# Four adaLN gate groups of the second layer: summed on VectorE in the first layer's output projection, not multiplied on TensorE in the second layer

## What is computed

```python
for l in range(DEPTH):
    last = l == DEPTH - 1
    shift, scale, gate = jnp.split(jax.nn.silu(c) @ ada_w[l] + ada_b[l], 3, axis=-1)
    shift_c, scale_c, gate_c = jnp.split(jax.nn.silu(c_ctx) @ ada_w[l] + ada_b[l], 3, axis=-1)
    h = rmsnorm(x, norm_g[l]) * (1.0 + scale[:, None]) + shift[:, None]
    hc = rmsnorm(xc, norm_g[l]) * (1.0 + scale_c) + shift_c
    ...                       # projections, attention, pooling, Fourier mixing
    x_new = x + gate[:, None] * out
    if not last:
        ...
        xc = xc + gate_c * outc
    x = x_new
```

## Time and profile before

| | |
|---|---|
| median of 3 runs | 2350.83 us (2349.53 to 2353.44) |
| span of the profiled execution | 2348.8 us |
| TensorE busy (matmul) | 2272.0 us, 97% |
| VectorE busy | 1288.4 us, 55% |
| ScalarE busy | 1042.1 us, 44% |
| GpSimd busy | 269.0 us, 11% |
| DMA | 437.14 MB, mean 186 GB/s |

### The profile page before, as it was taken

One profiled execution on the slowest core, in us unless ns is written; L12 is line 12 of the kernel. 1 busy time (PEld: TensorE's weight loads), 2 busy tenths in 40 slices (PEclk: granted clock), 3 DMA queues, 4 the chain that ended last, 5 costly groups with the idle time before them and its releaser, 6 DMA issues.

```text
span 2348.8 us, 30025 instructions
## 1 busy us (share of the span) xinstructions
PE 2272.0 (97%) x11859; PEld 1830.4 (78%) x11859; DVE 1288.4 (55%) x2030; ACT 1042.1 (44%) x1596; POOL 269.0 (11%) x326
## 2 busy tenths in 40 slices
PE   5899999999999999999999998999999999999998
PEld 2477777777777867678888887888888888888887
DVE  3354523332332264555776776667765777567764
ACT  2233333332322255445554565555544555345553
POOL 1010100000010122100020324111100111001111
PEclk9999999999999999999999998999999999999999
DMA  9974433445655475634566544565655555555553
GB/s 350 341 263 157 149 126 114 139 132 167 243 179 172 134 276 194 237 96 159 181 207 204 172 143 153 179 196 180 189 195 190 187 185 184 198 188 188 188 189 116
DMA packets 322427, 437.14 MB, mean 186 GB/s; under 512 B 13848, under 2 KB 220112, under 8 KB 321264
## 3 DMA queue, kind: packets, MB, share of 16 engines
q1 hardware_dynamic: 316800, 413.19, 53.2%
q0 software_dynamic: 3392, 16.90, 1.9%
q10 hardware_dynamic: 2096, 5.15, 0.6%
HBM read 428.89 MB, written 6.29 MB: 185 GB/s over the span
## 4 chain that ended last, share of the span: by engine, by line
PE 87%; DVE 4%; ACT 3%; DMA 3%; issue 1%; POOL 1%; SPq 0%; ACTq 0%; POOLq 0%
PE ps L1334 24%; PE ps L1335 12%; PE ps L1309 9%; PE ps L1311 8%; PE ps L1310 8%; PE ps L1329 5%; PE ps L1330 5%; PE ps L1331 5%; PE ps L1289 3%; PE ps L1383 1%; DVE SPL L1784 1%; ACT SPL L1540 1%; PE ps L1400 1%; DMA RAW<-in_ada_w_dram 1%; PE ps L1390 1%
## 5 line engine op out<-in xcount | busy, mean ns | idle before, releaser
L1784 DVE TENSOR_TENSOR SPL<-RAW,SPL 128x1024 fp32r<-128x1024 f32 x592 | 751.6, 1274 | 598.4 <-ACT SPL L1540 596.1
L1334 PE MATMUL ps<-HS,SPL 128*128 128x512 f32 x2688 | 957.7, 401 | 10.8 <-DVE SPL L1784 7.8
L1540 ACT ACTIVATE SPL<-RAW 128x1024 fp32r<-128x1024 f32 x592 | 622.1, 1055 | 493.2 <-PE ps L1311 170.9
L1335 PE MATMUL ps<-HS,SPL 128*128 128x256 f32 x2688 | 755.3, 281 | 0.0
L1334 PEld LDWEIGHTS ps<-HS,SPL 128*128 128x128 f32 x2688 | 507.7, 189 | 135.4 <-DVE SPL L1784 5.6
L1335 PEld LDWEIGHTS ps<-HS,SPL 128*128 128x128 f32 x2688 | 510.5, 190 | 2.0 <-issue 1.7
L1309 PE MATMUL ps<-SPL,HS 128*128 128x512 f32 x960 | 396.8, 413 | 12.2 <-DVE SPL L1784 5.3
L1311 PE MATMUL ps<-SPL,HS 128*128 128x512 f32 x960 | 377.1, 393 | 0.0
L1310 PE MATMUL ps<-SPL,HS 128*128 128x512 f32 x960 | 376.9, 393 | 0.0
L1309 PEld LDWEIGHTS ps<-SPL,HS 128*128 128x128 f32 x960 | 182.1, 190 | 75.5 <-issue 17.5
L1310 PEld LDWEIGHTS ps<-SPL,HS 128*128 128x128 f32 x960 | 182.3, 190 | 41.8 <-issue 6.3
(11 more groups left out here) (281 smaller groups left out, 1689.3 us busy)
## 6 DMA issues: line engine op xcount, KB each, us to landing
RAW<-in_w_in_dram SPq DMA_DIRECT2D x208, 512.0 KB, 5.7
RAW<-in_ada_w_dram SPq DMA_DIRECT2D x192, 512.0 KB, 4.9
RAW<-in_ffn_w_up_dram SPq DMA_DIRECT2D x192, 512.0 KB, 3.5
RAW<-in_w_out_dram SPq DMA_DIRECT2D x96, 512.0 KB, 4.5
RAW<-in_ffn_w_down_dram SPq DMA_DIRECT2D x96, 512.0 KB, 4.1
x_spill<-XT POOLq DMA_DIRECT2D x2, 2048.0 KB, 15.3
XT<-x_spill POOLq DMA_DIRECT2D x1, 4096.0 KB, 17.4
MM<-in_x_dram ACTq DMA_DIRECT2D x2, 1024.0 KB, 10.8
```

The costliest lines, as they stand in the source:

```text
L1334: mm(PS[b][:, :], wr, hh, start=k == 0, stop=False, skip_group_check=True)
L1335: m = mm(PS[b][:, 256:512], wl, hh[:, 0:256], start=False, stop=k == KT - 1, skip_group_check=True)
L1540: act(SPL[:, (n - 1) % NSPL, 0, :], raw_of(i), ACT.Copy).then_inc(s_hi, 1)
L1784: tt(w[:, 1, :], raw_of(s["i"]), w[:, 0, :].bitcast(F32), ALU.subtract).then_inc(s_lo, 1)
```

## The change

Groups 8 to 11 of layer 1 (the gates) become chunks of a new kind, shape 1, laid out among the chunks of `outs0[:28]`: from the fifth main chunk on, behind each main chunk one of them, two where the main chunk's number divides by 3; 32 in all. The adaLN chunks that were there stay. For such a chunk TensorE does nothing. VectorE multiplies each of its two k-halves by the column of silu(c) and adds it into one of two accumulators of 128 x 512, which lie in the first 1024 columns of `MM` (steps `ada_sum`). When a group is complete, four one-column matmuls of its accumulator with ones give the columns (`sum_turn`), and VectorE adds the bias. Only the latent gate is computed; the context's is not needed. In layer 1 the main chunks follow each other with no adaLN chunk between. Some semaphores of the two layers are merged, and the count of multiplied chunks (`s_chunk`) is kept apart from the position. `NRAW` stays at 8.

```diff
+        ACC = MM[:, 0:1024].rearrange("p (a c) -> p a c", a=2)
...
             while at["loaded"] < len(queue):
                 i = at["loaded"] - NRAW
                 last = []
-                if i >= 0 and queue[i].shape:
-                    if i >= at["taken"]:
+                if i >= 0:
+                    if i >= at["taken" if queue[i].shape else "pos"]:
                         return
-                    last = [(s_lo, split_no[i])]
-                elif i >= 0:
-                    if i >= at["pos"]:
-                        return
-                    last = [(s_chunk, i + 1)]
+                    last = [(s_lo, split_no[i])] if queue[i].shape > 1 else [after_chunk[i]]
...
                 i = at["taken"]
-                if queue[i].shape:
+                if queue[i].shape == 1:
+                    add_products(i, queue[i])
+                elif queue[i].shape:
                     if at["split"] - at["used"] >= NSPL:
                         return
...
+        def add_products(i, c):
+            g, half = c.group, c.group.half
+            put("ada_sum", i=i, kc=c.kc, half=half, before=at["summed"], last=acc_last[half] if c.kc == 0 else [])
+            at["summed"] += 2
+            after_chunk[i] = (s_acc, at["summed"])
...
                 c = chunks[i]
+                if c.shape == 1:
+                    at["pos"] = i + 1
+                    if c.then:
+                        c.then()
+                    continue
...
+        def ada_sums(l, g):
+
+            half = g % 2
+
+            def after():
+                sums = (s_acc, at["summed"])
+
+                def turn():
+                    s = put("sum_turn", l=l, g=g, half=half, sums=sums, after=use(7), out=tick("ada_out_columns"))
+                    acc_last[half] = [(s_accT, s["n"])]
+                    ada_ready[l, g] = (s_ada, s["out"])
+                    bank_last[7] = [ada_ready[l, g]]
+                while len(hi) < 8:
+                    hi.append(idle)
+                hi.insert(8, turn)
+
+            cs = group("sum", "ada", I["ada_w"][l, :, :], g * 512, [], after, side=0)
+            cs[0].group.half = half
+            acc_last[half] = [(s_m2, KT)]
+            return cs
...
-        left = [c for g in range(8, 12) for c in ada_group(0, g)] + [c for g in range(12) for c in ada_group(1, g)]
+        left = [c for g in range(8, 12) for c in ada_group(0, g)] + [c for g in range(8) for c in ada_group(1, g)]
+        gates1 = [c for g in range(8, 12) for c in ada_sums(1, g)]
...
-        lay_out(mixed(outs0[:28], left) + outs0[28:])
+        seq, mains = [], 0
+        for c in mixed(outs0[:28], left):
+            seq.append(c)
+            mains += c.shape > 0
+            if c.shape and mains > 4 and gates1:
+                n = 2 if mains % 3 == 0 else 1
+                seq.extend(gates1[:n])
+                del gates1[:n]
+        assert not gates1
+        lay_out(seq + outs0[28:])
         lay_out(left[:FILL])
         del left[:FILL]
-        lay_out(mixed(main1[1], left))
-        lay_out(mixed(outs1, left))
+        lay_out(main1[1])
+        lay_out(outs1)
...
+                elif kind == "sum_turn":
+                    e.wait_ge(*s["sums"])
+                    for b in range(4):
+                        m = mm(PS[7][:, b:b + 1], ACC[:, s["half"], b * 128:(b + 1) * 128], ONES[:, 0:1], start=True, stop=True, skip_group_check=True)
+                    m.then_inc(s_accT, 1)
...
+                elif kind == "ada_sum":
+                    i, kc, acc = s["i"], s["kc"], ACC[:, s["half"], :]
+                    for sm, v in new((s_c, 1), *s["last"]):
+                        e.wait_ge(sm, v)
+                    e.wait_ge(s_raw[i % NRAW], 16 * (i // NRAW + 1))
+                    for kk in range(2):
+                        w, c = raw_of(i)[:, kk * 512:(kk + 1) * 512], CW[:, 4 * kc + 2 * kk:4 * kc + 2 * kk + 1]
+                        if kc == 0 and kk == 0:
+                            ts(acc, w, c, None, ALU.mult).then_inc(s_acc, 1)
+                        else:
+                            e.wait_ge(s_acc, s["before"] + kk)
+                            stt(acc, w, c, acc, ALU.mult, ALU.add).then_inc(s_acc, 1)
```

More of the change, by code:

```diff
@@ L176, in two_block_program @@
         s_raw = [sem(f"raw{i}_in") for i in range(NRAW)]
-        s_tab, s_dft = [sem(f"rope{l}_in") for l in range(2)], [sem(f"dft{l}_in") for l in range(2)]
-        s_ap = [sem(f"pool_matrix{l}_in") for l in range(2)]
+        s_tab, s_dft = sem("rope_in"), sem("dft_in")
+        s_ap = sem("pool_matrix_in")
         s_map = [[sem(f"group_map{l}_{i}_in") for i in range(2)] for l in range(2)]
@@ L231, in two_block_program @@
         slots = [(i, []) for i in range(4)]
-        at = {"loaded": 0, "taken": 0, "split": 0, "used": 0, "pos": 0, "ahead": AHEAD}
+        at = {"loaded": 0, "taken": 0, "split": 0, "used": 0, "pos": 0, "ahead": AHEAD, "multiplied": 0, "summed": 0}
+        after_chunk, acc_last = {}, {}
         split_no, chunk_split = {}, {}
@@ L246, in multiplied @@
         def multiplied():
-            return (s_chunk, at["pos"])
+            return (s_chunk, at["multiplied"])
         def tm_aps(W, c0):
@@ L257, in group @@
             aps = fm_aps(W, c0) if form == "fm" else tm_aps(W, c0)
-            cs = [Chunk(g, kc, ap, {"ada": 0, "tm": 2, "fm": 4}[form]) for kc, ap in enumerate(aps)]
+            cs = [Chunk(g, kc, ap, {"ada": 0, "sum": 1, "tm": 2, "fm": 4}[form]) for kc, ap in enumerate(aps)]
             cs[-1].then = then
@@ L286, in run_ahead @@
                     split_no[i], chunk_split[at["split"]] = at["split"], i
-                    last = [(s_chunk, chunk_split[at["split"] - NSPL] + 1)] if at["split"] > NSPL else []
+                    last = [after_chunk[chunk_split[at["split"] - NSPL]]] if at["split"] > NSPL else []
                     put("split", i=i, last=last)
@@ L380, in spread @@
             def spread(slot):
-                s = put("ada_turn", slot=slot, l=l, g=g, after=use(7))
+                s = put("ada_turn", slot=slot, l=l, g=g, after=use(7), out=tick("ada_out_columns"))
                 give(slot, (s_adaT, s["n"]))
-                ada_ready[l, g] = (s_ada, s["n"])
+                ada_ready[l, g] = (s_ada, s["out"])
                 bank_last[7] = [ada_ready[l, g]]
@@ L1129, in two_block_program @@
         x1["rs"][0] = rstd_b(2, slot, 5)
-        x1["room"] = lambda k, s: [(s_chunk, marks[1] - 3 + 2 * s + k // 8)]
+        x1["room"] = lambda k, s: [(s_chunk, last_four + 1 + 2 * s + k // 8)]
         begin_h1()
@@ L1238, in two_block_program @@
                 put("mm", i=first + kc, c=chunks[first + kc], inputs={k: need["down", 2](k) for k in ks}, after={}, banks=[t], end=t == 1, src=None)
-                at["pos"] += t
-                at["used"] += t
+                if t:
+                    chunk_multiplied(first + kc)
             ready = rows_sum(3, t, alt(3)[t], multiplied() if t else (s_part, tick("part")))
@@ L1422, in tensor @@
                     lv, gi = lay[s["l"]], s["gi"]
-                    for sm, v in new(*s["ready"], (s_dft[s["l"]], 16)):
+                    for sm, v in new(*s["ready"], (s_dft, 16 * (s["l"] + 1))):
                         e.wait_ge(sm, v)
@@ L1432, in tensor @@
                     lv = lay[s["l"]]
-                    for sm, v in new((s_ap[s["l"]], 16 * 5)):
+                    for sm, v in new((s_ap, 16 * 5 * (s["l"] + 1))):
                         e.wait_ge(sm, v)
@@ L1820, in vector @@
                         c = c_norm + 16 * l + 4 * (g - 4)
-                        e.wait_ge(s_ada, n)
+                        e.wait_ge(s_ada, s["out"])
                         stt(S2[:, l, 4 * (g - 4):4 * (g - 3), :], a, 1.0, VV[:, c:c + 4].unsqueeze(2).to_broadcast([P, 4, 2]), ALU.add, ALU.mult).then_inc(s_s2, 1)
+                elif kind == "ada_sum":
[10 more added lines that the diff above has]
+                            stt(acc, w, c, acc, ALU.mult, ALU.add).then_inc(s_acc, 1)
+                elif kind == "sum_turn":
+                    l, g = s["l"], s["g"]
+                    c = c_adb + 48 * l + 4 * g
+                    for sm, v in new((s_col, 3)):
+                        e.wait_ge(sm, v)
+                    e.wait_ge(s_accT, n)
+                    tt(ADA[:, l, 4 * g:4 * g + 4, 0], PS[7][:, 0:4], VV[:, c:c + 4], ALU.add).then_inc(s_ada, 1)
                 elif kind == "h0":
```

28 lines of the change are left out of this document (17 added, 11 removed).

## The result

The changed kernel takes 2371.87 us (median of 4, 2371.44 to 2372.67) against 2351.49 us for the kernel before (median of 4, the three runs of the table above and one more): a ratio of 1.0092, 95% interval 1.0079 to 1.0106. It is 20 us slower. The forecast was 2349.6 us, range 2341 to 2358. The profiled execution has a span of 2370.9 us against 2348.8.

The account below looks back on a forecast made before the run. TensorE, busy 97% of the span, was taken as the bound. Cost 14.4 us minus gain 15.6 gave -1.2; with the 2348.8 us span and 2.0 us around it, 2349.6 us, range 2341 to 2358 (8 in 10).

Parts of the forecast that it names:

- The cost in the output projection: First layer's output projection: added sums cost 14.4 us through late splits, lower clock, extra TensorE work; bounds 10.9 and 21.
- The two holes: Output projection, behind main chunks 12 and 24: TensorE waits for splits placed after the residual addition, 3.9 us each, 7.8 together.
- turns: Output projection: four groups' sums become columns by one-column matmuls on TensorE's path, 0.86 us each, 3.4 us in all.
- the tail: End of the output projection: second tail chunk's split slips behind the last residual addition, 0.6 us.
- The clock: Output projection, after each of two TensorE waits: work at 1.2 GHz loses 1.3 us, 2.6 us together; bounds 0 and 3.4.
- the slow rival: Output projection, behind chunks 8 and 20: sums delay the next splits, 1 to 2 us each plus clock; chance 0.24.
- The gain in the second layer: Second layer: removing 32 adaLN chunks, their turns, copies and waits saves 15.6 us; bounds 9 and 22.
- The other nine count whole, 9.0 us: Second layer: of 11 adaLN pairs on the chain, two count half and nine save their full TensorE time, 9.0 us.
- the rival for a larger gain: Second layer: four main splits ahead and no raw-place waits also remove early holes; gain 19 to 22 us, 2344.7 us; chance 0.20.
- The largest single item: Second layer, near 985 us: TensorE's wait for the last adaLN group's addition goes, 2.9 us plus 0.9 of clock, 3.8 us.
- the first turn of the query norm: Second layer, norm of the first query group: TensorE arrives sooner and waits some 2 us for VectorE.
- VectorE late at more boundaries: Output projection waits behind chunks 8 and 20, with only 10 us gained in the second layer: 2357.2 us; chance 0.24.

Follow-up runs that it names:

- g1_late_turns: Changed kernel with seven positions ahead in the output projection, three for layer two's first 32 main chunks, four accumulators, sums' turns moved later: 2348.82 us, 0.9988 of before.

## Why the prediction was wrong, point by point

**The cost in the output projection: right in mechanism, short in size.** Forecast 14.4 us, measured 19.7. The two holes stand behind chunks 12 and 24, as worked out, and their positions were the cause (the moved double sums show it). Term by term: holes 7.8 us, measured 3.8 + 4.6 = 8.4; turns 3.4 us, measured 3.6; the tail 0.6 us, measured 0.8.

The clock was the term that was mis-sized: 2.6 us forecast, 2.7 + 2.3 = 5.0 measured. I took the losses from the two stretches of the earlier trace rows, and both stretches end while the clock is still low. The trace of the kernel before goes on:

```profile
1412.97 0.39 PE L1334 MATMUL ps<-HS,SPL 128*128 128x512 f32 x1
...
1421.01 0.77 PE L1334 MATMUL ps<-HS,SPL 128*128 128x512 f32 x1 [4.75 <-DVE SPL L1784]
...
1426.71 0.40 PE L1334 MATMUL ps<-HS,SPL 128*128 128x512 f32 x1
```

From 1408.87 to 1412.97 us seven pairs of matmuls take 4.1 us; at full clock a pair takes 0.35, together 2.4. That is 1.7 us lost, not 0.9. From 1421.01 to 1426.71 nine pairs take 5.7 us instead of 3.1: 2.6 us lost, not 1.7. With these the same reasoning would have given 4.3 us.

The rest is the short waits ahead of chunks 10 and 22, 1.4 + 0.4 us, behind the group ends at 8 and 20. I had them only in the slow rival, at these two places: 1.66 + 4 x 0.72 + 1.23 us left a margin of 0.7 us, but the four sums took 4.9 us there instead of 2.9. In all: 8.4 + 5.0 + 3.6 + 0.8 + 1.8 = 19.6 us.

The Trainium skill's page "TensorE: Matmul & The Clock Gate", section "Wait — 56ns, not 53.3ns?", gives a floor for the distance of two matmuls, and at that floor the four turns would cost an estimated 0.8 us. The trace shows 3.6, with each record loading its own stationary operand, as the earlier trace rows had it.

**The gain in the second layer: the step that failed.** Forecast 15.6 us with bounds of 9 and 22; measured -0.6, so 16.2 us are missing. Two things are in it. The kernel with three positions ahead gives the second of them, 9.2 us; 7.0 us are left for the first, and no kernel takes that one by itself.

The first is the sentence "The other nine count whole, 9.0 us". I read the chain as if a piece on it were worth its length. It is worth that only until the next chain is as long, and side chains were close behind almost everywhere. The kernel with thin adaLN matmuls takes 12 us out of TensorE at the same places and the stretch shrinks by 1.3. The clock belongs here as well: I took 1.0 us off for it, and the slow starts counted above come to some 5.

The second I had the wrong way round: "four main splits are ahead instead of two or three" stood in the rival for a larger gain. It was the loss. Five positions hold two or three main chunks where adaLN chunks lie between and four, all the split places, where they don't; the fourth split waits for a place, and ScalarE and VectorE wait with it, before tables, squares and norms that TensorE needs. With three positions the same kernel gains 9.2 us in the stretch. I had worked through the look ahead with care for the output projection, where the change adds chunks, and not for the second layer, where it takes them away; it is the same line of the planner.

**The largest single item**, the 3.8 us at the third attention step, went as forecast at its own place: TensorE no longer waits for the adaLN column (the wait of the earlier trace rows is in no list of after). From the first attention step to the end of the stretch, though, before took 56.1 us and after 58.1: waits of 1.8 and 1.0 us for ScalarE stand at the first steps now. A wait that goes lets TensorE run up to the next one.

**Near misses.** That the first turn of the query norm would wait some 2 us: it waited 3.2. That loads fit: they did. The rival "VectorE late at more boundaries" foresaw the slow side and 2357.2 us, and its two waits came, 1.8 us of the 20; its decision point, a gain in the second layer that falls short of the cost by 4.7 us, was passed by far, and for another cause.

**The sum as it was:** 19.7 + 0.6 = 20.3 us in the two stretches, beside a measured difference of 20.4 us in the medians (22.1 between the two profiled executions).

## What to carry to other kernels

A look ahead counted in positions of a mixed list changes its depth in the unit that matters whenever the mix changes; recount it at every place the change touches, where chunks are taken out as well as where they are put in. On an in-order engine a split that must wait for TensorE's place costs everything behind it, and a split that comes after a step waiting for TensorE is late; together they cost more here (16.0 and 9.2 us of the stretches) than the 18.0 us of TensorE's work that was moved. Before counting removed TensorE time as gain, ask at each place how far behind the next chain is; thinning the operation and keeping the order measures that, with what the clock takes in it. And when a loss at the lower clock is read from a trace, read on until the clock is back.

## What the runs showed of the hardware

- A scalar_tensor_tensor of 128x512 with one operand from a just landed buffer took 751 ns in the median and up to 1771 ns while GpSimd added, against 690 ns for the like in the earlier trace rows.
- After holes of 3.7 and 4.6 us TensorE lost 2.7 and 2.3 us to the lower clock level; in the kernel before, after 2.6 and 4.8 us, 1.7 and 2.6. That is half to three quarters of the hole, and the longest hole does not have the largest loss.
- Shorter holes did it at times. In the second layer after the change, matmuls 0.43 us apart follow the waits of 1.86 us at 843.43 us and 2.14 us at 921.23 us. In the kernel before, the same wait of 1.86 us at 823.15 us is followed by matmuls 0.23 us apart, and so is that of 1.34 us at 828.62 us.
- One-column float32 matmuls with a new stationary operand each cost 0.11 us a record at the full clock, and 0.21 us behind the hole of 4.89 us in g1_late_turns, at a mean granted clock of 0.50.
